# Seven-product form for half of the rows of the attention in-projection

## What is computed

```python
h = x * (1.0 + scale) + shift            # scale, shift, gate from c
proj = h @ w_in                          # 1024 x 1024 times 1024 x 10240
q, k, v (3 groups of 16 heads), gate_a = proj
scores, softmax, values per group; groups merged by their denominators
y = merged * silu(gate_a)
x = LayerNorm(alpha * x + gate * (y @ w_out))
```

## Time and profile before

| | |
|---|---|
| median of 3 runs | 2168.78 us (2166.26 to 2169.51) |
| the profiled execution, its span | 2173.1 us |
| TensorE busy | 2074.4 us, 95% |
| VectorE, ScalarE, GpSimd busy | 1051.4, 963.3, 826.5 us |
| DMA, read from and written to HBM | 195.75 and 24.19 MB |

### The profile page before, as it was taken

The page is one execution under the profiler, slowest core; times in us unless marked ns, Lnnn a source line. Parts: engine busy times, 40 slices in busy tenths (PEclk is TensorE's granted clock), DMA queues, the critical chain, the costliest instruction groups (busy, mean ns, idle before and its releaser), DMA issues.

```text
span 2173.1 us, 32149 instructions
## 1 busy us (share of the span) xinstructions
PE 2074.4 (95%) x11075; PEld 1653.5 (76%) x11075; DVE 1051.4 (48%) x2381; ACT 963.3 (44%) x2357; POOL 826.5 (38%) x436
## 2 busy tenths in 40 slices
PE   5999999999999999999999989899999999998997
PEld 4787887888878878878877777677777777776886
DVE  5522323223232233222333477788488488488553
ACT  3333433334334343333334345575475475485320
POOL 1211141221411413214114182476376375386472
PEclk9999999999999999999999999999999999999998
DMA  8412121221212212112221341655365265367431
GB/s 294 136 40 69 42 84 50 60 68 40 68 66 56 73 39 70 63 35 68 68 67 43 111 151 43 146 164 159 101 173 157 95 175 146 100 198 229 169 117 39
DMA packets 106242, 221.19 MB, mean 102 GB/s; under 512 B 18979, under 2 KB 53411, under 8 KB 105637
## 3 DMA queue, kind: packets, MB, share of 16 engines
q1 hardware_dynamic: 106148, 219.98, 33.6%
HBM read 195.75 MB, written 24.19 MB: 101 GB/s over the span
## 4 chain that ended last, share of the span: by engine, by line
PE 73%; DVE 10%; issue 5%; POOL 4%; ACT 4%; DMA 3%; SPq 1%; DVEq 0%; ACTq 0%; POOLq 0%
PE pp L535 39%; PE pp_s L2036 8%; PE tp L567 4%; PE sp_ L557 4%; PE yo_p L2240 3%; PE op L640 2%; PE pp_s L2240 2%; DVE stage_s L2666 2%; DMA w_raw_s<-in_b_w 2%; DVE vv L2602 2%; PE st_p L2240 1%; PE fill L2240 1%; PE op L629 1%; POOL trunk L1945 1%; PE tp L576 1%
## 5 line engine op out<-in xcount | busy, mean ns | idle before, releaser
L467 POOL TENSOR_TENSOR w_lo<-w_raw,w_hi 128x1024 fp32r<-128x1024 f32 x79 | 191.0, 2418 | 833.9 <-ACT w_hi L813 833.9
L535 PE MATMUL pp<-h_hi,w_hi 128*128 128x512 f32 x1232 | 488.6, 397 | 0.0
L535 PE MATMUL pp<-h_hi,w_lo 128*128 128x512 f32 x1232 | 480.3, 390 | 0.0
L535 PE MATMUL pp<-h_lo,w_hi 128*128 128x512 f32 x1232 | 479.7, 389 | 0.0
L1091 DVE COPY probT<-tp 128x512 f32<-128x512 f32 x160 | 103.2, 686 | 544.6 <-PE tp L567 544.6
L2036 PE MATMUL pp_s<-h_hi,w_hi_s 128*128 128x512 f32 x624 | 268.8, 431 | 20.4 <-DVE stage_s L2666 14.3
L535 PEld LDWEIGHTS pp<-h_hi,w_hi 128*128 128x128 f32 x1232 | 231.4, 188 | 49.4 <-issue 4.3
L535 PEld LDWEIGHTS pp<-h_hi,w_lo 128*128 128x128 f32 x1232 | 231.2, 188 | 49.5
L535 PEld LDWEIGHTS pp<-h_lo,w_hi 128*128 128x128 f32 x1232 | 231.6, 188 | 45.5
L874 ACT ACTIVATE prob<-prob,mz 128x256 f32<-128x256 f32 (+2 forms) x384 | 170.4, 446 | 191.7 <-DVE mz L1071 191.7
L2036 PE MATMUL pp_s<-h_hi,w_lo_s 128*128 128x512 f32 x624 | 245.8, 394 | 1.9 <-issue 1.9
(11 more groups left out here) (458 smaller groups left out, 3606.6 us busy)
## 6 DMA issues: line engine op xcount, KB each, us to landing
w_raw<-in_a_w SPq DMA_DIRECT2D x80, 512.0 KB, 3.3
rw<-cum_rows SPq DMA_DIRECT2D x32, 1024.0 KB, 6.3
w_raw_s<-in_b_w SPq DMA_DIRECT2D x40, 512.0 KB, 4.0
ew<-exp_rows SPq DMA_DIRECT2D x64, 256.0 KB, 7.3
num_wide<-in_ada_w SPq DMA_DIRECT2D x16, 768.0 KB, 6.5
num_wide<-merge_rows SPq DMA_DIRECT2D x16, 768.0 KB, 7.8
num_wide<-in_ada_w SPq DMA_DIRECT2D x20, 512.0 KB, 6.2
yT_b<-trunk SPq DMA_DIRECT2D x32, 256.0 KB, 2.4
```

What stands on the lines that cost most here:

```text
L467: nc.gpsimd.tensor_tensor(lo.rearrange("p k c -> p (k c)"), w_raw[:, slot].rearrange("p k c -> p (k c)"), hi.rearrange("p k c -> p (k c)") ...
L535: last = nc.tensor.matmul(pp[:, par, :], w[:, slot, k, :], keep[h][:, k, half * HALF:(half + 1) * HALF], start=(k == 0 and n == 0), stop=( ...
```

## The change

The eight rows of 128 of the contraction are parted: four stay plain, the other four are taken as 2 x 2 blocks (two blocks of two rows, two halves of the tokens) against two tiles of weights, and computed with seven block products instead of eight. Two tiles are now a unit. The seven forms of `h` (A11, A12, A22 and four sums) are made once, before the loop: GpSimd sums, ScalarE rounds, VectorE makes the rest. For each unit GpSimd makes the sums of the weights, T2, T3 and T4, and changes two slots of raw weights in place (`early`, `late`); ScalarE rounds them (`round_r1`, `round_t23`, `round_r2`, `round_t4`); TensorE computes the first step of a unit with 36 matmuls and the second with 54 (`first_half`, `second_half`, banks b0, b1, b2); VectorE adds the products up in nine operations (`first_sums`, `second_sums`), a bank's sum or two buffers `ua` and `va`. The plain part of the first tile's second token half stands at the head of the second step. Four tiles (three before, one after `h` is there) stay plain; unit 0 comes before the loop, five are in each pair, two in the last.

Since b2 takes a bank, `op` has one bank instead of two, and `values` waits for the `numerators` before it. The forms of `h` lie where the merged tiles of `y` were: `merge` now writes into `wide`, SyncE stores each pair's tile to HBM, and the last pair loads them back (`store_y`, `load_y`). x is loaded row by row into a ring of four. The gate's sum is made as a column in eight products, and its weighings on VectorE come after the first value copies. VectorE takes the differences of the statistics before the last sum of step 9 and the shares after it; ScalarE's part comes before the next pair's begin. `evacuate` keeps its forms. In the last pair tile 0's output products move from steps 5 to 8 into 6 to 8. In the code below 12 leading blanks are cut.

```diff
+KS = 2
+PL = KT - 2 * KS
...
+LAST_DUOS = ((VT2, Q2), (K2, GATE))
+FIRST_DUO = (Q1, K1)
+PLAIN = 4
+NT_UNITS = 1 + 5 * (PAIRS - 1) + 2
+EVENTS, SUMS = 9, 9
...
+    def load_unit(n):
+
+        if isinstance(n, int) and n == 0:
+            sp.wait_ge(lo_done, PLAIN - 1)
+            load(PLAIN, 0)
+            sp.wait_ge(lo_done, PLAIN)
+            load(PLAIN + 1, 1)
+            return
+        sp.wait_ge(t_made, 2 * n)
+        for i in range(2):
+            load(PLAIN + 2 * n + i, i)
...
+    def early(n):
+
+        pool.wait_ge(w_in[0], 16 * n + 48)
+        pool.wait_ge(w_in[1], 16 * n + 48)
+        if not isinstance(n, int) or n:
+            pool.wait_ge(pp_full, PP_FULL + EVENTS * n - EVENTS + 4)
+        t2, t3 = (t_raw[:, i] for i in range(2))
+        nc.gpsimd.tensor_tensor(t3, w_raw[:, 1, B_Y, :], w_raw[:, 1, B_X, :], ALU.subtract)
+        link(n, nc.gpsimd.tensor_tensor(w_raw[:, 1, B_X, :], w_raw[:, 1, B_X, :], w_raw[:, 0, B_X, :],
+                                        ALU.subtract), 1)
+        nc.gpsimd.tensor_tensor(t2, w_raw[:, 1, B_Y, :], w_raw[:, 1, B_X, :], ALU.subtract
+                                ).then_inc(t_made, 1)
+        pool.wait_ge(w_rounded, 4 * n + 1)
+        rest(w_lo[:, 0], w_raw[:, 0], w_hi[:, 0]).then_inc(w_ready, 1)
+        pool.wait_ge(w_ready, 4 * n + 1)
+        link(n, nc.gpsimd.tensor_tensor(w_raw[:, 0, B_Y, :], w_raw[:, 0, B_Y, :], w_raw[:, 1, B_Y, :],
+                                        ALU.subtract), 2)
+        pool.wait_ge(w_rounded, 4 * n + 2)
+        rest(t_lo[:, 0:2], t_raw[:, 0:2], t_hi[:]).then_inc(w_ready, 1)
+
+    def late(n):
+
+        pool.wait_ge(w_rounded, 4 * n + 3)
+        rest(w_lo[:, 1], w_raw[:, 1], w_hi[:, 1]).then_inc(w_ready, 1)
+        if not isinstance(n, int) or n:
+            pool.wait_ge(pp_full, PP_FULL + EVENTS * n)
+        nc.gpsimd.tensor_tensor(t_raw[:, 2], w_raw[:, 0, B_Y, :], w_raw[:, 1, B_X, :],
+                                ALU.add).then_inc(t_made, 1)
+        pool.wait_ge(w_rounded, 4 * n + 4)
+        link(n, rest(t_lo[:, 2], t_raw[:, 2], t4_hi), 3)
+        pool.sem_inc(w_ready, 1)
+
     def weigh(j, g):
         if g == 0:
             pool.wait_ge(wide_in, 32 * j + 32)
-        pool.wait_ge(o_free, 10 * j + 2 + (4, 8, 10)[g])
+        pool.wait_ge(o_free, DUOS * j + 1 + (4, 8, 10)[g])
...
     with pool.Fori(0, PAIRS - 1) as j:
-        for f in range(4, 13):
-            split_lo(10 * j + (6 + f), f % 2)
+        for i in range(3, 7):
+            early(5 * j + i)
+            late(5 * j + i)
+        early(5 * j + 7)
         for g in range(3):
             weigh(j, g)
-        split_lo(10 * j + 19, 1)
+        late(5 * j + 7)
         merge(j)
...
+    def passes(bank, weights, hs_, begin, end):
+
+        (w1, w2), (h1, h2) = weights, hs_
+        for i, (w, h) in enumerate(((w1, h1), (w1, h2), (w2, h1))):
+            last = nc.tensor.matmul(bank, w, h, start=begin and i == 0, stop=end and i == 2)
+        return last
+
+    def product(bank, weights, form, begin=False, end=False):
+
+        for i in range(KS):
+            last = passes(bank, [w[:, i, :] for w in weights], [h[:, form, i, :] for h in hs],
+                          begin and i == 0, end and i == KS - 1)
+        return last
...
+    def first_half(n):
+
+        first = isinstance(n, int) and n == 0
+        pe.wait_ge(w_ready, 4 * n + 1)
+        pe.wait_ge(pp_free, PP_FREE + 4 * n - 1)
+        product(b0, rows_of(0, B_X), A11, begin=True, end=True).then_inc(pp_full, 1)
+        if first:
+            pe.wait_ge(pp_free, PP_FREE)
+        product(b1, rows_of(0, B_Y), A12, begin=True)
+        plain(b1, 0, 0, end=True).then_inc(pp_full, 1)
+        pe.wait_ge(w_ready, 4 * n + 2)
+        pe.wait_ge(pp_free, PP_FREE + 4 * n)
+        if first:
+            pe.wait_ge(h_lo, KT + 1)
+        product(b2, T2, S2, begin=True, end=True).then_inc(pp_full, 1)
+        pe.wait_ge(comb, SUMS * n + 1)
+        if first:
+            pe.wait_ge(h_lo, KT + 2)
+        product(b0, T3, S3, begin=True, end=True).then_inc(pp_full, 1)
+
+    def second_half(n, between=None):
+
+        pe.wait_ge(comb, SUMS * n + 3)
+        plain(b2, 0, 1, begin=True).then_inc(pp_full, 1)
+        pe.wait_ge(w_ready, 4 * n + 4)
+        product(b2, T4, A22, end=True).then_inc(pp_full, 1)
+        pe.wait_ge(pp_free, PP_FREE + 4 * n + 1)
+        if isinstance(n, int) and n == 0:
+            pe.wait_ge(h_lo, KT + 4)
+        product(b1, rows_of(1, B_X), S1, begin=True, end=True).then_inc(pp_full, 1)
+        pe.wait_ge(comb, SUMS * n + 4)
+        plain(b0, 1, 1, begin=True, end=True).then_inc(pp_full, 1)
+        if between:
+            between()
+        pe.wait_ge(pp_free, PP_FREE + 4 * n + 2)
+        product(b2, rows_of(1, B_Y), S4, begin=True)
+        plain(b2, 1, 0, end=True).then_inc(pp_full, 1)
 
     def scores(j, d):
 
         g, n0, nt = duo_of(d)
         if d == 0:
-            pe.wait_ge(pp_free, 20 * j + 8)
+            pe.wait_ge(pp_free, 6 if isinstance(j, int) and j == 0 else 20 * j + 4)
         if d == 4:
-            pe.wait_ge(pp_free, 20 * j + 14)
+            pe.wait_ge(pp_free, 20 * j + 12)
...
             for i in range(2):
                 for h in range(2):
                     c = probT[:, h, :].rearrange("p (t i c) -> p i t c", t=2, i=2)
-                    last = nc.tensor.matmul(op[HD * h:HD * h + HD, d % 2, 0:2 * P],
+                    last = nc.tensor.matmul(op[HD * h:HD * h + HD, 0:2 * P],
...
+    for half in range(2):
+        transpose_v(half, half, half, 2)
+    pe.wait_ge(lo_done, PLAIN)
+    for half in range(2):
+        pe.wait_ge(pp_free, half + 1)
+        for k in range(KT):
+            last = passes(pp[:, half, :], [w[:, 1, k, :] for w in (w_hi, w_lo)],
+                          [h_of(i, k, half) for i in range(2)], k == 0, k == KT - 1)
+        last.then_inc(pp_full, 1)
+    first_half(0)
+    for half in range(2):
+        transpose_v(2 + half, half, half, PP_FREE)
+    scores(0, 0)
+    second_half(0)
+    pe.wait_ge(g_used, KT)
+    pe.wait_ge(pp_free, 4)
+    gate_products()
+    pe.wait_ge(n_used, KT)
+    pe.wait_ge(t_free, T0 + 2)
+    next_sums(0).then_inc(ncol_full, 1)
...
+    def stretch(j, d, table):
+
+        if d:
+            new_v(j, d - 1, table)
+            duo_values(j, d - 1, table)
+        if d < DUOS - 1:
+            scores(j, d + 1)
+        new_probs(j, d, table)
...
+            n = 5 * j + (d // 2 + 1)
+            stretch(j, d, T_AT)
             if d == DUOS - 1:
                 scores(j + 1, 0)
-                n = T_AT[("s", 0)]
-                transpose_stats_and_sum(j, NT * j + (T0 + n), n % 2)
-            proj(j, 10, 2 * d, range(4))
-            if d == DUOS - 1:
-                duo_values(j, d, T_AT)
-            proj(j, 10, 2 * d + 1, range(4))
+                at = T_AT[("s", 0)]
+                transpose_stats_and_sum(j, NT * j + (T0 + at), at % 2)
+                second_half(n, lambda: duo_values(j, DUOS - 1, T_AT))
+            elif d % 2:
+                second_half(n)
+            else:
+                first_half(n)
...
+    def begin_pair(j, before, kinds):
+
+        second_tile(j - 1 if before else j, 5 * j, DUOS_OF_TILES[4] if before else FIRST_DUO, 0)
+        if before:
+            nc.scalar.activation(qscale[:], qscale[:], ACT.Copy, scale=2.0).then_inc(scale_set, 1)
+            act.wait_ge(scale_set, j)
+        round_r2(5 * j + 1)
+        if before:
+            numerators(j - 1, DUOS - 1)
+        round_t4(5 * j + 1)
+        softmax(j, 2)
+        softmax(j, 3)
+        first_tile(j, 5 * j + 1, kinds, 0)
...
-            weights_at(j, d + 1)
-            numerators(j, d - 1)
+            n = 5 * j + (d // 2 + 1)
+            kinds = DUOS_OF_TILES[d // 2]
+            if d % 2:
+                if d > 1:
+                    numerators(j, d - 1)
+            else:
+                second_tile(j, n - 1, DUOS_OF_TILES[d // 2 - 1], 0)
+                round_r2(n)
+                numerators(j, d - 1)
+                round_t4(n)
             if d < DUOS - 1:
                 softmax(j, 2 * d + 2)
                 softmax(j, 2 * d + 3)
             else:
                 softmax(j + 1, 0)
                 softmax(j + 1, 1)
-            unit(j, 2 * d, STEP_TILES, T_AT)
-        unit(j, 19, STEP_TILES, T_AT)
-        nc.scalar.activation(qscale[:], qscale[:], ACT.Copy,
-                             scale=2.0).then_inc(scale_set, 1)
-        act.wait_ge(scale_set, j + 1)
-        first_duo(j + 1, True)
+            if d % 2:
+                round_r1(n + 1)
+                first_tile(j, n, kinds, 1)
...
+    def first_sums(n):
+
+        dve.wait_ge(pp_full, PP_FULL + EVENTS * n + 1)
+        if not isinstance(n, int) or n:
+            dve.wait_ge(comb, SUMS * n)
+        nc.vector.tensor_copy(ua, b0).then_inc(comb, 1)
+        dve.wait_ge(pp_full, PP_FULL + EVENTS * n + 2)
+        dve.wait_ge(comb, SUMS * n + 1)
```

(52 more changed lines are left out.)

568 lines of the change are left out of this document (335 added, 233 removed).

## The result

The changed kernel takes 2156.34 us (median of 4, 2154.93 to 2157.34) against 2167.52 for the kernel before in the same group (median of 4): ratio 0.994, 95% interval 0.9921 to 0.9959, 11.2 us faster. In a later group it was 2155.77 against 2172.05: 0.9924 (0.9910 to 0.9939), 16.3 us. The forecast was 39.4 us and 2129.4. The direction is right, the size is not.

The account below looks back on a forecast made before the run. TensorE was taken to bound the kernel, busy 2074.4 of 2173.1 us. Matmuls -51.7, loop +7, start +7.3 and end -2 sum to -39.4 us, from 2168.8 to 2129.4 us; range 2112 to 2158.

Parts of the forecast that it names:

- the term of -51.7: Projections on TensorE: 38 units save 6 matmuls each, 228 at an unchanged spacing of 0.2267 us, -51.7 us.
- The layout of the loop: Hand-made timeline of a unit and the merge chain in a pair, from which TensorE's waits in the loop were forecast.
- S4 of step 7: Tightest regular step of the loop: slack shrinks to 0 to 0.4 us; 0.1 us a pair taken.
- The fourth rival: Loop: the merge weights' broadcast lands late and TensorE waits once a pair; 2173 to 2210 us, middle 2185, chance 0.08.
- the start, +7.3: Before and around unit 0: waiting for the first copy +6.4, weighings for the next layer +1.8, gate sums -0.9.
- T3's wait: Unit 0: TensorE waits for VectorE's first copy behind gate rows and remainders of forms, +6.4 us, between 0 and 11.
- The gate sums as eight columns: Start: gate sums, 1.81 us as four products, become eight of one column, -0.9 us.
- the loop, +1.0 a pair: Three waits of TensorE in a pair add to 0.7 us; +1.0 taken, +7 us in all, between 2 and 25.
- values 1: Step 2 of a pair: TensorE waits until numerators 0 are copied from the single output bank; 0.2 us, between 0 and 2.5.
- the state-space half: The kernel's other half, said not to be touched by the change; 0 us.
- The end, -2: Last pair's steps without projections, paced by GpSimd's remainders of the output weights: -2 us, between -6 and +5.
- the second one: Every unit waits, as VectorE or ScalarE must answer nine times in order; 2140 to 2164 us, middle 2150, chance 0.20.

Follow-up runs that it names:

- vector_rotated: The changed kernel with VectorE's loop over pairs cut at another place, where it waits for TensorE anyway; 2151.65 us, 0.991 of the kernel before.
- kept_busy: The changed kernel with 44 wide matmuls that nobody reads filling TensorE's wait before T3 of unit 0; 2150.22 us, 0.9905 of the kernel before.
- the second pair: Both kernels run and traced again without edits: before 2171.7 us (1.0002), span 2169.0; changed 2155.77 us (0.9924), span 2151.8.

## Why the prediction was wrong

**Right.** The count and the spacing: 18 matmuls take 4.08 us on the chain, 0.2267 each, and the term of -51.7 stands. GpSimd's remainders of the weights stayed at 2414 ns beside the new sums, against 2418, and the straight line (0.73), not the row of 0.91, gave the operations of 256 columns: the one below takes 733 ns, four others 749 to 787 and one 878:

```profile
L556 POOL TENSOR_TENSOR w_lo<-w_raw,w_hi 128x1024 fp32r<-128x1024 f32 x76 | 183.4, 2414 | 367.6 <-ACT w_hi L1032 367.6
L586 POOL TENSOR_TENSOR h_forms_raw<-w_raw 128x256 f32<-128x256 f32 x38 | 27.8, 733 | 151.2 <-DMA w_raw<-in_a_w 80.2 <-PE pp L673 71.0
```

The layout of the loop: the next weights were to be rounded 18.5 us after the last unit (409.50), the remainder to end at 21.0, the weighing at 25.6, numerators 0 to be copied at 26.1, TensorE to arrive at 25.9. They came at 18.6, 21.1, 25.7, 26.2 and 25.7. To the tenth that is partly luck: without the standstill at the turn of VectorE's loop, in `vector_rotated`, the same points lie at 18.2, 20.6, 25.3 and 25.7, so the layout was 0.4 us long and the standstill, which it did not have, made that up. The stalls stand where they were placed, and S4 of step 7 waits 0.1 to 0.7 us in the two traces of the changed kernel in place of 0 to 0.4. The fourth rival, the late broadcast, did not occur.

**Wrong: the start, +7.3 against +17.7.** This term makes 10.4 of the 19.5 us missing between the first traces, 8.0 of 22.2 between the second. Four sizes in it failed (10.6 us in all, by single readings).
- T3's wait, 6.4 against 10.97 (its upper bound was 11). "Four remainders of the new forms (1.28 each, as the weighings)": they took 2.12, and two gate rows 2.36. Both kinds read two SBUF operands while GpSimd works, and take turns with it. The step that failed: the contention of VectorE and GpSimd was weighed in the prediction for the sums with PSUM, where it costs nothing (2414 ns), and not for the instructions that read two SBUF operands; the four remainders, all on the way to T3, were priced from rows of 1.28 with GpSimd idle. The trace of the kernel before could have settled it: of its seven L518, the last (1297.45) took 2.39 us with VectorE idle, and six took 3.26 to 3.39 beside a scalar_tensor_tensor or tensor_tensor of VectorE. The last row's end, 103.5, is also 1 us later than the prediction's own terms give (96.5 + 4.7 + 1.28 = 102.5); it came at 108.7.
- The clock was in no term. An idle stretch was priced as its length alone; behind it the same matmuls took 2.6 us more (6.2 against 3.6 in kept_busy), and behind the second, at 0.73, 1.5 more (3.6 against 2.1): 4.1 us.
- The gate sums as eight columns, -0.9: they take 1.84 us against 1.81, no gain.
- TensorE reached the first transposes 1.0 us later than the row of before it was laid from; eight of the thirteen later traces with the changed projection, and one of the kernel before, were 4 to 5 us earlier there, so this is scatter.

**Too low: the loop, +1.0 a pair against 1.64.** The idle time is 0.97 in the pair shown, of which 0.56 before values 1 (0.2 forecast), and there the mechanism was another: VectorE's standstill at the turn of its loop. Cutting the loop elsewhere gave back 0.4 us a pair. The other 0.6 or so is spread over the pair and not placed.

**Left out: the state-space half, 0 against +3.5 and +9.3.** "The state-space half is not touched" took the same text for the same time. Behind the first st_p matmul the changed kernels take 5.7 us more on average; some 4 go with the loops' place in the code, the rest stays open.

**The end, -2 against -0.9.** Idle time there is about what it was, but 5.9 us run at 0.50 (1170.60 on).

**The rivals.** The measured time lies in the second one's range, and yet not by its mechanism: the units after the first make TensorE wait at three places of a pair (before values 1, before S4 of step 7, and 0.17 us before the first transposes), not nine times a unit, and the start's loss went away with unit 0. The time fits; the trace does not.

**The base.** 19.9 us between the first traces, 11.2 between the first medians, 17.2 and 16.3 in the second pair: so the disagreement of the first pair, some 8 us, was mostly the kernel before scattering.

## What to carry to other kernels

Price the one unit ahead of a loop on its own: its engines are full of other work, and there the saving of 1.4 us was bought with the largest loss of the attention phase; with it plain the kernel is some 15 us faster. VectorE instructions with two SBUF operands beside a working GpSimd are priced with GpSimd's instruction ahead of them, and moving them to GpSimd slows those that stay. When TensorE is made to wait, add what the clock takes behind the wait. Code that is not changed can still take another time when it stands elsewhere. When instructions are added to a loop or to what stands ahead of it, look at the instruction queue's packets, and cut the loop where its engine waits anyway.

## What the runs showed of the hardware

- A VectorE instruction with two SBUF operands and one of GpSimd took turns: on VectorE a remainder of 1024 columns took 1.2 us with GpSimd idle and up to 3.41 with it working, ending 1.1 us behind GpSimd's instruction; GpSimd's own, of 512 columns, took 1.34 on average and 2.15 beside VectorE. VectorE's sums with one operand in PSUM left GpSimd's 1024 columns at 2414 ns.
- VectorE's loop of 358 instructions loaded code at each turn and stood still for 2.7 to 3.1 us, at both places where it was cut; the loop of 233 stood 0.2 to 0.3 us. A later loop of 387 was turned in 0.12 us, so length alone doesn't decide. Packets of that queue are about 8 KB.
- 55 to 92 added waits (two waits to an instruction) cost 0.11 us an instruction on VectorE.
- ScalarE's standstill of 2.5 us at the turn of its state-space loop (372 instructions) went when the loop was moved by 78 instructions, and came in the kernel before when it was moved by 50 (and VectorE's by 55). The same state-space code took some 4 us less of 840 on average with its loops moved; the two groups touch.
- After 11 us without work TensorE ran at 0.54 of its clock for 6.2 us, and 22 matmuls took 2.6 us longer; with filler matmuls in that gap it stayed at 1.00, whatever the DMA share.
